# Tables inside the first block, first weights handed from block to block, and another order of first loads and downs

## The reference

```python
def _half_ffn(x, g, w_gate, w_up, w_down):
    h = _rmsnorm(x, g)
    return x + 0.5 * ((jax.nn.silu(h @ w_gate) * (h @ w_up)) @ w_down)

    xp = _half_ffn(xp, g_ffn1[l], w1_gate[l], w1_up[l], w1_down[l])
    q_p, kv_p = proj(_rmsnorm(xp, g_mix[l]))
    o_p = _query_blocks(lambda qb, pb: mix(*qb, pb, *kv_p, pos_p), q_p, pos_p)
    xp = xp + o_p @ w_out[l]
    xp = _half_ffn(xp, g_ffn2[l], w2_gate[l], w2_up[l], w2_down[l])
...
    # the same for the sample rows xs, whose keys follow a cache of 512
```

## Time and profile before

| | |
|---|---|
| runs | 2956.0, 2949.03, 2954.74 us; median 2954.74 |
| profiled execution | 2956.32 us, its span 2954.4 |
| PE busy | 2577.7 us, 87% of the span |
| DVE, ACT, POOL busy | 51%, 31%, 5% |
| mean granted clock of PE | 0.945 of the upper level |

### The profile page before, as it was taken

One profiled execution on the slowest core, in us unless ns is written; L12 is line 12 of the kernel. 1 busy time (PEld: TensorE's weight loads), 2 busy tenths in 40 slices (PEclk: granted clock), 3 DMA queues, 4 the chain that ended last, 5 costly groups with the idle time before them and its releaser, 6 DMA issues. The chain is left out here.

```text
span 2954.4 us, 38232 instructions
## 1 busy us (share of the span) xinstructions
PE 2577.7 (87%) x14986; PEld 2276.5 (77%) x14986; DVE 1510.0 (51%) x3003; ACT 915.1 (31%) x1535; POOL 159.8 (5%) x259
## 2 busy tenths in 40 slices
PE   5999999895889889998796778889999687999998
PEld 4899899895677777798664766767778587998997
DVE  3444444542677655553432588886555224344443
ACT  2222222321444333332212375653333112222221
POOL 0000000221010000031000000010000000000000
PEclk9999999997899999999898888999999888999999
DMA  5222222344433333342633423332221321222221
GB/s 164 93 72 72 72 72 72 109 142 128 121 97 98 99 84 86 100 133 79 182 110 117 132 63 95 95 84 74 72 68 61 117 94 43 72 72 72 72 72 65
DMA packets 332354, 274.95 MB, mean 93 GB/s; under 512 B 30960, under 2 KB 300688, under 8 KB 331536
## 3 DMA queue, kind: packets, MB, share of 16 engines
q1 hardware_dynamic: 332176, 272.52, 30.9%
HBM read 227.41 MB, written 34.83 MB: 89 GB/s over the span
## 5 line engine op out<-in xcount | busy, mean ns | idle before, releaser
L1005 ACT ACTIVATE c_w_hi<-c_w_raw 128x2048 fp32r<-128x2048 f32 x37 | 70.5, 1904 | 198.7 <-PE c_result L895 128.0
L1005 ACT ACTIVATE a_w_hi<-a_w_raw 128x2048 fp32r<-128x2048 f32 (+1 forms) x43 | 81.5, 1895 | 151.2 <-PE a_result L895 128.0
L842 PE MATMUL a_result<-a_w_hi,a_XTh 128*128 128x256 f32 (+1 forms) x400 | 114.9, 287 | 2.7 <-issue 1.5
L844 PE MATMUL a_result<-a_w_hi,a_XTl 128*128 128x256 f32 (+1 forms) x400 | 113.6, 284 | 0.0
L843 PE MATMUL a_result<-a_w_lo,a_XTh 128*128 128x256 f32 (+1 forms) x400 | 113.6, 284 | 0.0
L873 PE MATMUL c_gate<-c_XTh,c_w_hi 128*128 128x320 f32 x352 | 110.1, 313 | 1.5 <-DVE c_XTl L1173 1.5
L873 PE MATMUL a_gate<-a_XTh,a_w_hi 128*128 128x320 f32 x352 | 110.0, 312 | 1.5 <-DVE a_XTl L1173 1.5
L874 PE MATMUL c_gate<-c_XTl,c_w_hi 128*128 128x320 f32 x352 | 109.9, 312 | 0.0
L875 PE MATMUL c_gate<-c_XTh,c_w_lo 128*128 128x320 f32 x352 | 109.9, 312 | 0.0
L875 PE MATMUL a_gate<-a_XTh,a_w_lo 128*128 128x320 f32 x352 | 109.9, 312 | 0.0
L874 PE MATMUL a_gate<-a_XTl,a_w_hi 128*128 128x320 f32 x352 | 109.9, 312 | 0.0
(11 more groups left out here) (445 smaller groups left out, 7853.6 us busy)
## 6 DMA issues: line engine op xcount, KB each, us to landing
a_w_raw<-in_w_gate SPq DMA_DIRECT2D x22, 512.0 KB, 4.0
a_w_raw<-in_w_up SPq DMA_DIRECT2D x22, 512.0 KB, 5.4
a_w_raw<-in_w_down SPq DMA_DIRECT2D x11, 1024.0 KB, 4.9
m_w_raw<-in_w_gate SPq DMA_DIRECT2D x22, 512.0 KB, 4.0
m_w_raw<-in_w_up SPq DMA_DIRECT2D x22, 512.0 KB, 5.3
m_w_raw<-in_w_down SPq DMA_DIRECT2D x11, 1024.0 KB, 5.0
h_w_raw<-in_w_gate SPq DMA_DIRECT2D x22, 512.0 KB, 4.0
h_w_raw<-in_w_up SPq DMA_DIRECT2D x22, 512.0 KB, 5.4
```

What stands on the lines that cost most here:

```text
L842: pe.matmul(out, XTh[:, i, tok], hi[:, i], start=(i == 0), stop=False)
L844: last = pe.matmul(out, XTl[:, i, tok], hi[:, i], start=False, stop=(i == KD - 1))
L1005: act.activation(w_hi[:, c % 2, 0:n], w_raw[:, c % 2, 0:n], ACT.Copy).then_inc(hi_split, 1)
```

## The change

- **Tables.** `load_and_tables` is gone. Its work is inside block a: SP loads the bucket rows after the first chunks and the gains; DVE spreads the table at step 6; PE makes one lookup behind `dense(k)` in each of steps 8 to 19, all into one bank `look_bank`, which DVE frees by its copy a step later; SP stores each a step after that; lambda is made at steps 22 to 24. The near tables are loaded and stored at steps 30 and 42, before at 10 and 22. `R_BANKS` is 3 in a and c, before 4.
- **Weights handed on.** `w_raw`, `w_hi` and `w_lo` are made once for all blocks. A block has `following`, and loads and splits the first two chunks of the next one at its own end; the next one begins with `GIVEN` = 2 chunks ready.
- **Rows.** In c `rows` has five slots and all five loads are issued at once, ahead of everything else. In h it has one as before.
- **First loads.** In m and h SP issues the first queries, the indexer's keys, the next queries, `double(0)`, then x (h) and the gain, chunks 2 and 3, and after them the gains of m, keys, values and near tables, and in h the remaining rows.
- **Order on PE.** In the first six steps (`FRONT`) of m and h `dense` comes ahead of `attend`. The first gate and up products wait for the norm of the tiles of their own part (three tiles for the first part of a and c), before for all.
- **Downs.** Of the first tile of a pair the products with hidden block 0 come first, for both halves, then those with the upper part of hidden block 1, then those with its lower part. The waits are for the first part alone; the second part is waited for at the tile where it begins.
- `sample_attention` uses buffers of its own twice, to make room.

```diff
-    R_BANKS = 2 if ATT else 4
+    R_BANKS = 2 if ATT else 3
+    FRONT = 6
+    LAST_CHUNK = N_CHUNKS + (2 if following else 0)
     def load_step(c):
-        return 0 if c < 2 else split_step(c - 2) + 2
+        return 0 if c < GIVEN + 2 else split_step(c - 2) + 2
-        ROW_SLOTS = 1 if mode == "out" else 2
+        ROW_SLOTS = (1 if ATT else NE) if mode == "out" else 2
...
                 if mode == "out":
-                    load_rows(0)
+                    for t in range(ROW_SLOTS):
+                        load_rows(t)
...
-                load_chunk(0)
-                if ATT:
                     load_queries(1)
-                load_chunk(1)
+                    double(0)
                 if mode == "out":
                     for t in range(NE):
                         load_x(t)
...
-                else:
+                load_chunk(GIVEN)
+                load_chunk(GIVEN + 1)
+                if mode == "in":
...
                 if ATT:
-                    double(0)
                     load_diff_keys(0)
...
-                        if b == 0:
-                            pe.wait_ge(result_taken, R_PAIR)
-                            pe.wait_ge(xt_hi, T_NORM + 2 * NE)
+                    if w == 0 and b == 0 and contraction[0] == 0:
+                        tiles = -(-(part + 1) * PART // P)
+                        pe.wait_ge(result_taken, R_NORM + 2 * tiles)
+                        pe.wait_ge(xt_hi, T_NORM + 2 * tiles)
...
-                    if t == 0:
-                        pe.wait_ge(lo_split, c + 1)
-                        pe.wait_ge(hid_lo, N_PART * (2 * i + 2))
+                    chunk_split(pe, c)
+                    pe.wait_ge(hid_lo, N_PART * 2 * i + 1)
                     for half in range(2):
+                        with_hi(half, 0)
+                        with_lo(half, 0)
+                    pe.wait_ge(hid_hi, N_PART * (2 * i + 1) + 1)
+                    for half in range(2):
+                        with_hi(half, 1)
+                    pe.wait_ge(hid_lo, N_PART * (2 * i + 1) + 1)
+                    for half in range(2):
+                        with_lo(half, 1)
...
                 for k in range(STEPS):
-                    if ATT:
+                    if ATT and k >= FRONT:
                         attend(k)
                     if k < N_UNITS:
                         dense(k)
+                    if ATT and k < FRONT:
+                        attend(k)
+                    if windows and 0 <= k - LOOK < HEADS:
+                        pe.wait_ge(spread, 1)
+                        if k > LOOK:
+                            pe.wait_ge(vec_ready, k - LOOK)
+                        pe.matmul(look_bank[:, 0:SKEW], table_b[:, k - LOOK, :], onehot[:], start=True, stop=True).then_inc(looked_up, 1)
```

More of the change, by code:

```diff
@@ L407, in bank @@
             return ctx.enter_context(nc.psum_tensor(name, shape, F32))
+        if windows:
+            look_bank = bank(tag + "_looked_up", [P, 512])
         if ATT:
@@ L421, in merged @@
         x_loaded = [sem(f"{tag}_x_loaded{n}") for n in range(NE)]
-        rows_loaded = sem(tag + "_rows_loaded")
+        rows_loaded = [sem(f"{tag}_rows_loaded{n}") for n in range(ROW_SLOTS if mode == "out" else 0)]
         in_done = sem(tag + "_in_done")
@@ L669, in _ @@
                 for k in range(STEPS):
-                    if mode == "out" and k + 1 < NE:
-                        load_rows(k + 1)
-                    for c in range(2, N_CHUNKS):
+                    if mode == "out" and k + ROW_SLOTS < NE:
+                        load_rows(k + ROW_SLOTS)
+                    for c in range(GIVEN + 2, LAST_CHUNK):
                         if load_step(c) == k:
@@ L880, in down @@
                     c = N_OUT + 3 * i + 2
[L881 to L896 removed]
+                    hi = w_hi[:, slot(c)].rearrange("p (j d) -> p j d", j=2)
@@ new lines, in down, with with_hi @@
+                    lo = w_lo[:, slot(c)].rearrange("p (j d) -> p j d", j=2)
+                    tok = slice(t * P, (t + 1) * P)
+                    first = R_PAIR + 2 * NE * i + 2 * t
+                    out = [r_bank[(first + half) % R_BANKS][:] for half in range(2)]
+                    def with_hi(half, j):
+                        cols = slice(half * 512, half * 512 + 512)
+                        if j == 0:
+                            pe.wait_ge(result_taken, first + half - R_BANKS + 1)
+                        pe.matmul(out[half], hid[:, j, tok], hi[:, j, cols], start=(j == 0), stop=False)
+                        pe.matmul(out[half], hid[:, j, tok], lo[:, j, cols], start=False, stop=False)
@@ new lines, in with_lo @@
+                    def with_lo(half, j):
+                        last = pe.matmul(out[half], hid[:, 2 + j, tok], hi[:, j, half * 512:half * 512 + 512], start=False, stop=(j == 1))
+                        if j == 1:
+                            last.then_inc(result_done, 1)
+                    if t:
+                        if N_PART == 2 and t == PART // P:
+                            pe.wait_ge(hid_lo, N_PART * (2 * i + 2))
+                        for half in range(2):
+                            for j in range(2):
+                                with_hi(half, j)
+                                with_lo(half, j)
+                        return
@@ L986, in attend @@
                             turn(head_mixed_at[a - 1], 0)
+                if windows:
+                    pe.wait_ge(ident_ready, 1)
                 if ATT:
@@ L1487, in _ @@
                         take(u)
-                    for c in range(N_CHUNKS):
+                    for c in range(GIVEN, LAST_CHUNK):
                         if split_step(c) + 1 == k:
```

298 lines of the change are left out of this document (139 added, 159 removed).

## The result

The changed kernel takes 2848.2 us (median of 4 runs, 2842.0 to 2849.8) against 2951.9 for the kernel before (the three runs listed above and a fourth of 2948.83): a ratio of 0.9644, 95% interval 0.9623 to 0.9665. The forecast was 2855, range 2820 to 2900. The profiled execution has a span of 2848.0, which is 106.4 less than before; the sum of the forecast was 100.0.

The account below looks back on a forecast made before the run. The prediction took PE, busy 87% of the span, as the bound, so only its waits could be won. Its terms summed to −100.0 us from the profiled 2956.3, giving 2856.3 and a median of about 2855, range 2820 to 2900.

Parts of the forecast that it names:

- Part 1: Start of block a: tables moved inside a let its loads start earlier, lookups cost +9; sum −16.6 us (−17.7 to −9.6).
- Part 2: Downs of a and c: the 1.65 wait goes, a 0.5 stall comes, a pair gains 1.15; −25.4 us (−36.4 to 0).
- Part 3: Downs of m and h: PE's waits shrink; −12 us in m (0 to −26), −8 in h (0 to −12).
- Part 4: Start of m: transposes fill PE's idle time, the scores' wait stays, first gate comes earlier; −6 us (0 to −11).
- Part 5: Start of h: row chain remains, scores and their wait leave the stretch before the first projection; −4 us (+3 to −12).
- Part 6: Start of c: five row slots, all loads issued at once, first projection after 13.9; about −23 us (−18 to −25).
- Part 7: Norm of c: five slots let scales come between takes, first gate about 14.2 after last take; −8.5 us (−5 to −13).
- Part 8: Block ends: loading and splitting the next block's two chunks costs +1.5 in a and m, +0.5 in h; +3.5 us (0 to +6).
- B: Rival: downs give nothing, since three banks and halves ending together make PE wait for VectorE; 2900 us, chance 0.13.
- E: Rival: slower, the third bank is missing throughout the downs of a and c; 2968 us at 0.8 a unit, chance 0.02.
- D: Rival: SP stops on `double(0)`, loads behind it come later, h starts 3 later, m no earlier; 2868 us, chance 0.05.
- C: Rival: clock falls vanish, fuller gains in all downs and at the starts of m and h; 2813 us, chance 0.15.

Follow-up runs that it names:

- the experiment: Changed kernel with the tables in a block of their own ahead of a, as before the change: 2854.4 us, ratio 0.9675.

## Why the prediction was right, and where its steps were not

**Part 1, the tables** (−16.6): the start held to 0.2 (−25.8 for −25.6). The lookups were mis-sized: about 12.7 by the experiment, 9 taken, inside the bounds. Halving the cold row gave 0.66 for one; it takes 0.93, and delays the product behind it by 0.1.

**Part 2, downs of a and c** (−25.4): mis-sized in its stall. Of 0.5 a pair, 0.05 is seen, and four banks bring 1.8 in c for eleven pairs. The step that failed is that half 2 "is taken 6.46–7.12": the second of two takes costs 0.60, not 0.69, and each record of VectorE begins 0.08 to 0.09 ahead of the end of the one before, where the sum put a gap. So half 2 is taken from 6.12 on and the bank is free at about 6.8, just when PE comes. The reading that "the first three tiles need only the first of two parts" is wrong as well: the third waits for the second part, at no cost seen here. The old order costs 16.6 and 19.3, 35.9 together. c has some 3 more from the clock behind its norm, and a some 1.4 at its first products (the first 49 took 9.7 us before and 8.3 after); no term named either.

**Part 3, downs of m and h** (−12, −8): the order alone gives m 8.5 to 11.9, a little under the term, and the table's −17.1 holds some 5 more, which are the clock's (the windows under the old order). In the edits that leave m's downs alone the stretch takes 480.0 to 483.7, with the lower clock for 28.3 us in the shortest and some 36 in the longest. h lost 9.1 by the old order, and its stretch is 5.8 shorter; with the old order PE waits 20.6 us for takes there, where the kernel before had 16.9. The Trainium skill, "TensorE: Matmul & The Clock Gate", section "HAM oscillation — how this bites in real kernels", has PE's gaps bring the clock down. What the prediction took from it, that the falls would go with the waits, is not borne out: they became fewer, but with the old order, which has the waits, as much as without.

**Part 4, start of m** (−6, measured −5.1): the size held by luck, the reason did not. The step that failed is "the scores' wait is not removed": the 11.0 us that PE stood there are gone, by the early doubles, and PE then stands on VectorE's scaled rows and splits (4.4, 6.5 and 2.7 us). Taking the parts out one at a time costs 1.8 (order on PE), 5.8 (early doubles) and 6.5 (weights handed on, of which the sum counted the two splits only beside it): each of the last two alone is more than the whole gain.

**Part 5, start of h** (−4, measured +0.3, and +2.3 behind it): wrong, and by the prediction's own sign ("a start of m, h or c is later than before"). It named the chain of rows through one slot and said "this chain remains", and yet took 4 off the 6.7 from the fourth row's turn to the first projection for scores moved out of the way. This stretch is 5.8 after (1597.73 to 1603.55): PE now waits there for VectorE's split of the turned row. The order on PE did bring the first turn from 24.3 to 4.2 us after the first load, by removing the 18.1 of the scores' wait, but the second row was issued as late as before, and PE stood 22.1 there. The experiments show that the chain's place in SP's order sets it (−19.6 when it is moved), and that the order on PE cost 5.5 in this block.

**Part 6, start of c** (−23, measured −24.7): the number was right and a sentence behind it was wrong: "The weights made ahead give nothing of their own here: they were ready long before the rows". They were ready before the rows *of the old order*. With all rows at once the weights come last, and the five slots alone win 3.4, or 11.2 with the chunks loaded ahead of x. So the handing on, priced "at nothing but its cost", is worth 13.5 to 21.4 at this start.

**Part 7, norm of c** (−8.5, measured −9.1): right. VectorE's order is as worked out, the scales 3.75 apart in the trace after. From the last take to the first gate it is 10.3 where the sign said 14; the last take itself comes 3.3 later after the first projection than before, so that the sum holds. The slots explain 7.2 of it.

**Part 8, ends** (+3.5): a +1.8, m +2.3, h 0; the two experiments without handing on give 3.0 and 2.5, and 0.8 and 3.9, back, so the sizes hold only roughly.

**The rivals.** B (three banks eat the downs) and E fall with the rows of c's pair. D is real but worth 1 to 2 in h, and the early doubles pay in m. SP stands from 1554.08 to 1557.56 ahead of the first double, and all loads behind it come after. The rule cited for D, that a wait is spent on the issuing sequencer (the Trainium skill, "DMA: Bandwidth & Descriptors", section "Anatomy of one DMA — SWDGE (gpsimd) path"), agrees with this, on SP's queue too. C's fuller gain came true in a and c only. That the total was so close is luck, since two errors met: by the table, stretches that came out 21.1 better than forecast (the pairs of c and m 14.4 of it) stand against 14.7 worse (h's start, norm and pairs 8.8, the sample block 3.9).

## What to carry to other kernels

When a change removes two things that wait for the same stretch, ask for each what the stretch would be with it alone: what is "ready long before" under the old order may be last under the new one. An engine that works in order stands at the first instruction whose data are late, whether or not anybody needs its result; look at what is queued behind it, and at the next late thing, to which the wait may only move. And when several loads share one issuing engine, find the chain that takes longest from its issue to its end, and issue that first.

## What the hardware showed beside this

The sample block has the same instructions in the changed kernel and in all edits, and took 195.5 to 201.6 us. Here it is in the changed kernel and in the one with h's rows early (stretch, us, busy of PE, PEld, DVE, ACT, POOL, clock, DMA share, GB/s):

```profile
1350.74:1552.34 201.60, 170.83 (x1022) 123.39 (x1022) 77.87 (x187) 41.13 (x110) 5.23 (x5) 0.87 0.37 111
```

```profile
1353.38:1548.92 195.54, 164.46 (x1022) 120.59 (x1022) 77.87 (x187) 41.06 (x110) 5.22 (x5) 0.91 0.38 114
```

Same counts, same VectorE and ScalarE time, a granted clock of 0.87 and 0.91, and PE busy 6.4 longer. Six microseconds of a difference between two programs can thus come from a block that neither of them touched. Nor need it be the program's: the four executions of the changed kernel itself lie between 2842.0 us at a mean granted clock of 0.955 and 2849.8 at 0.949, and the one profiled is the longest of them.

SP's issue of a single transfer takes 0.3 to 0.6 us for most of the 749 in the changed kernel, but 3.4 to 6.9 for seven of them, 5.23 for the near tables in h (row above). In such a stretch a load pays for the issues ahead of it as well.
